# Layer 1 MLP: last four block products of a pair's second product inside the next pair's first; layer 0 issues its sum transfers at the pairs' ends

## The reference, cut to what matters

```python
def _sq_relu_mlp(h, w1, w2):
    return jnp.square(jax.nn.relu(h @ w1)) @ w2
...
        h_lat = h_lat + g1 * y_lat
        h_lat = h_lat + g2 * _sq_relu_mlp(_modulate(_rms_norm(h_lat, norm2_g[i]), sh2, sc2), mlp_w1[i], mlp_w2[i])
        if not last:
            h_ctx = h_ctx + cg1 * y_ctx
            h_ctx = h_ctx + cg2 * _sq_relu_mlp(_modulate(_rms_norm(h_ctx, norm2_g[i]), csh2, csc2),
                                               mlp_w1[i], mlp_w2[i])
```

## Time and profile before

| what | value |
|---|---|
| median of 3 runs (2562.03 to 2565.29) | 2564.84 us |
| the profiled execution: its time, its span | 2568.6 us, 2567.1 us |
| PE busy | 2319.5 us, 90% of the span |
| DVE busy | 1731.1 us, 67% |
| ACT, POOL busy | 1155.4 us, 1155.5 us, 45% each |
| mean granted TensorE clock | 0.956 |
| layer 0's MLP, pairs 0 to 15 | about 320 to 1271 us |
| layer 1's MLP, loop over pairs 2 to 15 | about 1940 to 2547 us |

### The profile page before, as it was taken

One profiled execution on the slowest core, in us unless ns is written; L12 is line 12 of the kernel. 1 busy time (PEld: TensorE's weight loads), 2 busy tenths in 40 slices (PEclk: granted clock), 3 DMA queues, 4 the chain that ended last, 5 costly groups with the idle time before them and its releaser, 6 DMA issues. The chain is left out here.

```text
span 2567.1 us, 38476 instructions
## 1 busy us (share of the span) xinstructions
PE 2319.5 (90%) x11430; PEld 1908.2 (74%) x11430; DVE 1731.1 (67%) x2827; ACT 1155.4 (45%) x2117; POOL 1155.5 (45%) x974
## 2 busy tenths in 40 slices
PE   5989989999999999999789798989988999998988
PEld 3768768888888877888677677767767777777776
DVE  5643786766776766676674688871787676767675
ACT  5543433333333333333343488883444444444444
POOL 0004533333334444433546566665455554545453
PEclk9999989999999999999889899999989999999999
DMA  7434225555544555554512211105122222222222
GB/s 264 168 136 165 99 60 159 150 139 144 134 131 131 146 144 150 160 151 108 165 61 99 93 32 38 33 21 205 38 66 73 83 82 86 86 86 86 86 80 84
DMA packets 132197, 283.51 MB, mean 110 GB/s; under 512 B 11408, under 2 KB 19984, under 8 KB 128784
## 3 DMA queue, kind: packets, MB, share of 16 engines
q1 hardware_dynamic: 111776, 242.09, 28.1%
q0 software_dynamic: 17408, 33.56, 7.9%
q10 hardware_dynamic: 2928, 6.82, 0.7%
HBM read 265.64 MB, written 83.89 MB: 136 GB/s over the span
## 5 line engine op out<-in xcount | busy, mean ns | idle before, releaser
L881 POOL TENSOR_TENSOR ht<-ht,l_side 128x512 f32<-128x512 f32 x112 | 167.5, 1495 | 535.8 <-ACT l_side L1017 533.6
L51 PE MATMUL l_z_ps<-nh,l_w1h 128*128 128x512 f32 (+1 forms) x816 | 292.9, 359 | 6.6 <-POOL l_w1l L58 3.4
L53 PE MATMUL l_z_ps<-nh,l_w1l 128*128 128x512 f32 (+1 forms) x816 | 291.8, 358 | 0.0
L52 PE MATMUL l_z_ps<-nl,l_w1h 128*128 128x512 f32 (+1 forms) x800 | 285.8, 357 | 0.0
L1321 DVE SCALAR_TENSOR_TENSOR ht<-l_yy_ps,mod,ht 128x512 f32<-128x512 f32 x336 | 235.9, 745 | 20.6 <-PE l_yy_ps L1637 19.2
L2662 PE MATMUL l_yy_ps<-l_ah,l_w2h 128*128 128x512 f32 x448 | 190.2, 425 | 61.3 <-DVE ht L2491 61.1
L58 POOL TENSOR_TENSOR l_w2l<-l_w2f,l_w2h 128x512 fp32r<-128x512 f32 x128 | 181.4, 1467 | 108.9 <-ACT l_w2h L2157 105.1
L58 POOL TENSOR_TENSOR l_w1l<-early,l_w1h 128x512 fp32r<-128x512 f32 x104 | 135.6, 1311 | 179.7 <-ACT l_w1h L2149 179.7
L1635 PE MATMUL l_yy_ps<-l_ah,l_w2h 128*128 128x512 f32 x448 | 187.0, 417 | 22.3 <-ACT l_side L1017 14.6
L3389 POOL TENSOR_TENSOR sc<-sc,den 128x640 f32<-128x640 f32 (+1 forms) x128 | 149.5, 1200 | 91.8 <-DVE den L3471 91.8
L2664 PE MATMUL l_yy_ps<-l_ah,l_w2l 128*128 128x512 f32 x448 | 185.3, 414 | 0.0
(11 more groups left out here) (338 smaller groups left out, 6533.5 us busy)
## 6 DMA issues: line engine op xcount, KB each, us to landing
l_aw<-ada SPq DMA_DIRECT2D x128, 256.0 KB, 2.9
sums<-w SPq DMA_DIRECT2D x64, 512.0 KB, 7.8
maw<-ada SPq DMA_DIRECT2D x24, 1024.0 KB, 5.1
l_w1f<-w SPq DMA_DIRECT2D x32, 512.0 KB, 5.8
l_w2f<-w SPq DMA_DIRECT2D x32, 512.0 KB, 4.2
sums<-w POOLq DMA_DIRECT2D x32, 512.0 KB, 7.3
sums<-sums POOLq DMA_DIRECT2D x32, 512.0 KB, 5.9
l_w2f<-sums SPq DMA_DIRECT2D x64, 256.0 KB, 2.7
```

Of the source, the lines that this page charges most:

```text
L51: pe.matmul(out, lh, rh, start=first, stop=False)
L52: pe.matmul(out, lh, rl, start=False, stop=False)
L53: return pe.matmul(out, ll, rh, start=False, stop=last)
L881: pool.tensor_tensor(h, h, side[(i - 1) % 2][:], ALU.add).then_inc(s_add, 1)
```

## The change: what it does

Layer 0: POOL's list for a pair is reordered. `first_sums` stands at the pair's start, behind the "S4" transfer of the pair before; "S2" stands at the pair's end. After the last pair "S4" follows at once, and POOL waits for it as before.

Layer 1: the block products with the indices 3, 4, 5 of a pair run on PE behind the next pair's first-product blocks M1, M5 and M6, index 6 behind M4. The lists of the other engines follow. Operand and weight rings have new slots and release conditions (`W2_RING`, `W2_AFTER`, `A_AFTER`), the operand order is new, DVE splits four w2 blocks per pair where it split three and POOL three where it split four. The number of matmuls, `acc`, `diff` and `low` per pair is the same. The last pair's four late products run behind the loop.

```diff
@@ -923,18 +923,18 @@
                 def outputs(p, more):
+                    if C:
+                        if type(p) is not int or p:
+                            more_sums(p - 1, "S4")
+                        first_sums(p)
                     add(p, "M5")
                     low2(p, "S2")
                     add(p, "M3")
-                    if C:
-                        first_sums(p)
                     if more and C:
                         low1(p + 1, 0)
                     low2(p, "S3")
                     for prod in ROWS[2:]:
                         add(p, prod)
-                        if C and prod in ("M2", "M7"):
-                            more_sums(p, "S2" if prod == "M2" else "S4")
...
+                    if C:
+                        more_sums(p, "S2")
...
                 outputs(PAIRS - 1, False)
                 if C:
+                    more_sums(PAIRS - 1, "S4")
                     pool.wait_ge(s_s4, 16 * PAIRS)
...
-    ON_DVE2 = 3
-    A_ORDER = ["B11", "T2", "T3", "T1", "T4", "B22", "B21"]
+    W2_RING = [0, 1, 2, 0, 1, 0, 2]
+    W2_AFTER = [(1, 5), (1, 4), (1, 6), (0, 0), (0, 1), (0, 3), (0, 2)]
+    HIGH2, DVE2, POOL2 = [1, 0, 2, 3, 4, 6, 5], [1, 0, 6, 5], [2, 3, 4]
+    A_ORDER = ["B11", "T2", "T3", "B21", "T4", "T1", "B22"]
...
@@ -2484,53 +2536,87 @@
+                def pair_start(p):
+
+                    low(p - 1, "T1")
+                    acc(p - 1, 3)
+                    low2(p - 1, 6)
+                    low(p - 1, "B22")
+                    low2(p - 1, 5)
+                    acc(p - 1, 4)
+
+                def pair(p, earlier=True):
+                    if earlier:
+                        pair_start(p)
+                    low2(p, 1)
+                    if earlier:
+                        acc(p - 1, 5)
+                    low2(p, 0)
                     zsum(p, "B11")
                     square(p, "B11")
+                    zsum(p, "B22")
                     low(p, "B11")
-                    zsum(p, "B22")
                     square(p, "B22")
                     zsum(p, "B12")
                     square(p, "B12")
                     diff(p, "T1")
-                    last_sums(p, False)
+                    diff(p, "T2")
+                    if earlier:
+                        acc(p - 1, 6, (0, 1))
+                    square(p, "B21")
...
@@ -2682,10 +2774,14 @@
-                def pair(p):
-                    for prod in Z_ORDER:
+                def pair(p, earlier=True):
+                    for k, prod in enumerate(Z_ORDER):
                         hidden(p, prod)
-                    for i in (0, 1, 2, 3):
+                        if earlier and k < 3:
+                            product(p - 1, 3 + k)
+                    if earlier:
+                        product(p - 1, 6)
+                    for i in (0, 1, 2):
                         product(p, i)
```

More of the change, by code:

```diff
@@ L2050, in low_t, with pair @@
                     lo_part(pool, lo, t_full(t, j), hi).then_inc(s_tlo[t], 1)
[L2052 to L2067, removed]
+                def pair(p, more, earlier=True):
+                    low1(p, 3)
+                    if earlier:
+                        add(p - 1, 3)
+                    low1(p, 4)
+                    if earlier:
+                        add(p - 1, 4)
+                    low1(p, 5)
+                    if earlier:
+                        add(p - 1, 5)
+                    low1(p, 6)
                     if more:
@@ L2070, in pair @@
                         low1(p + 1, 2)
-                    rest(p, more)
+                        low1(p + 1, 0)
+                    if earlier:
+                        add(p - 1, 6)
+                    low2(p, 2)
+                    add(p, 0)
+                    low2(p, 3)
+                    add(p, 1)
+                    low2(p, 4)
+                    add(p, 2)
                 def low_p(w):
@@ L2096, in _ @@
                         low1(0, 2)
+                        low2(0, 2)
                 squares(UNITS - 1)
@@ L2117, in _ @@
                 low1(2, 1)
+                low2(1, 2)
+                add(1, 0)
                 low2(1, 3)
-                add(1, 0)
                 low1(2, 2)
+                add(1, 1)
                 low2(1, 4)
[L2122 to L2126, removed]
+                for i in (2, 3, 4, 5, 6):
                     add(1, i)
-                with pool.Fori(PLAIN, PAIRS - 1) as p:
+                pair(PLAIN, True, False)
+                with pool.Fori(PLAIN + 1, PAIRS - 1) as p:
                     pair(p, True)
                 pair(PAIRS - 1, False)
+                for i in (3, 4, 5, 6):
+                    add(PAIRS - 1, i)
             @block.scalar
@@ L2348, in _ @@
                     high_t("T3", j)
-                side_read(1, 3)
-                high2(1, 6)
                 for i in (4, 5, 6):
                     side_read(1, i)
-                with act.Fori(PLAIN, PAIRS - 1) as p:
-                    start(p, True)
-                    rest(p, True)
-                    for i in (4, 5, 6):
-                        side_read(p, i)
+                pair(PLAIN, True, False)
+                with act.Fori(PLAIN + 1, PAIRS - 1) as p:
+                    pair(p, True)
                 last = PAIRS - 1
-                start(last, False)
-                rest(last, False)
+                pair(last, False)
+                high2(last, 6)
+                side_read(last, 3)
+                high2(last, 5)
                 def out_half(i):
@@ L2498, in last_sums @@
                     low(p, "T3")
-                    acc(p, 0, 0)
-                    acc(p, 0, 1)
-                    if not (type(p) is int and p == 0):
+                    acc(p, 0, (0, 1))
+                    if p:
                         square(p, "B21")
                     diff(p, "T4")
+                    acc(p, 0, (2, 3))
+                    acc(p, 1, (0, 1))
+                    low(p, "B21")
+                    acc(p, 1, (2, 3))
+                    low(p, "T4")
                     low(p, "T1")
-                    acc(p, 0, 2)
@@ L2506, in last_sums @@
[L2506 to L2507 removed]
+                    acc(p, 2)
                     low(p, "B22")
[L2509 to L2520 removed]
@@ L2522, in pair @@
-                def pair(p):
-                    for i in (0, 1, 2):
-                        low2(p, i)
+                    low2(p, 6)
+                    acc(p, 3)
+                    if p:
+                        for j in range(HK):
+                            low_t("T1", j)
+                    low2(p, 5)
+                    acc(p, 4)
+                    acc(p, 5)
+                    if p:
+                        for t in ("T3", "T4"):
+                            for j in range(HK):
+                                low_t(t, j)
@@ L2582, in _ @@
                 square(1, "B22")
-                for j in range(HK):
-                    low_t("T4", j)
-                last_sums(1, True)
-                with dve.Fori(PLAIN, PAIRS) as p:
+                plain_rest(1)
+                pair(PLAIN, False)
+                with dve.Fori(PLAIN + 1, PAIRS) as p:
                     pair(p)
+                pair_start(PAIRS)
+                acc(PAIRS - 1, 5)
+                acc(PAIRS - 1, 6)
                 for i in range(len(HALVES)):
```

300 lines of the change are left out of this document (175 added, 125 removed).

## The result

The changed kernel takes 2538.02 us, median of 4 runs (2535.28 to 2538.97), against 2565.07 (2562.03 to 2568.72): a ratio of 0.989, 95% interval 0.9874 to 0.9906.

A forecast was written before the change was run, and what follows sets the result against it. PE, busy 90% of the span, was taken as the bound, with only its waits and slow clock to win. 2568.6 - 60 (layer 0) - 45 (layer 1) = 2463.6, less 3.8 for the median: 2460 us, range 2425 to 2520.

The forecast's parts named there:

- I take no change in PE's time: Layer 0: moved transfers run beside the `l_aw` loads without delaying PE, as about 2 us of slack cover them.
- the slower rival: Layer 0: the two-slot `l_aw` load chain becomes the bound of hidden; 2598 us at twice the present landing; chance 0.03.
- part of layer 0's gain is lost to the loads: Layer 0: moved transfers delay `l_aw` or weight loads; half of each wait kept gives 2496, a quarter 2478; chance 0.14.
- The price formula of that rival: Layer 0, per pair: four load rounds, each growing with the landing, less 2 us of slack; 9.2 us at twice the landing.
- 25.5 us of slow stretches: Layer 0: PE's slow matmuls behind the `low2` waits go with those waits, 15 times 1.7 us gained.
- Layer 0, what goes: Layer 0's pairs: PE's waits for `low2` (32.4 us) and `side_read` (14.6) and the slow stretches (25.5) vanish; gain 72.5 us.
- The end of layer 0: After layer 0's last pair: "S2" and "S4" follow each other unhidden, next stage 11 us later, bounds 6 and 17.
- Layer 1: Layer 1's loop: period falls to 40.6 us, 3.2 less, without a clock drop; 45 us saved, bounds 0 and 72.
- the walk: Layer 1, PE from M4 to index 2: three banks late by 1.4 us in all, from DVE operations of 0.66 us each.
- The extra split on DVE: Layer 1: one more `low2` per pair costs nothing, or 0.8 us per pair, 11 over the loop, through SBUF contention.
- The forecast of layer 0: Layer 0 in all: 72.5 us gained, 11 lost at its end, 1.5 for restarts and small waits; 60 us less.

The follow-up runs named there:

- l0_only: The kernel before with only POOL's new list in layer 0, layer 1 as before; 2587.51 us, ratio 1.0082.
- best1: `first_back` with `low1` of the next pair's first chunk ahead of `first_sums`, and "S2" and "S4" issued earlier in the last pair; 2440.75 us, ratio 0.953.
- first_back: The changed kernel with `first_sums` alone put back behind the add of M3, "S4" still at the pair's head; 2461.17 us, ratio 0.9589.
- l1_only: The changed kernel with POOL's old list in layer 0, so only layer 1 is new; 2510.56 us, ratio 0.979.
- best2: `best1` with DVE's `acc` of index 1 in layer 1 ahead of T4's difference and the `low` of B21; 2446.36 us, ratio 0.9541.
- best3: `best2` with ACT's `side_read` of index 1 ahead of the high part of B21; 2431.52 us, ratio 0.9484.
- serial: The changed kernel with POOL waiting for "S4" to land before it issues `first_sums`; 2486.64 us, ratio 0.9703.

## Why the prediction was wrong, step by step

- **The step that failed** is "I take no change in PE's time, since I put the end of these steps some 2 us ahead of the point where outputs need them". The 2 us were about right, the runs give 1.7. What was wrong is to take the delay of the chain (load, `ada_step`, next load) as less than that: DVE's waits for `l_aw` grew from 19.9 to 99.3 us, 5.7 us per pair, and PE waited 54.2 us, 3.9 per pair, with a slow stretch behind each of 14 waits. In the pair shown the slow matmuls behind 655.31 (0.42 us against 0.23) cost about 1.6 us; in seven of 13 pairs the slow stretch is about twice as long.
- The mechanism stood in the prediction twice: as the slower rival, with 0.03, and in milder form as "part of layer 0's gain is lost to the loads", with 0.14, which ended at 2496. What was wrong is the weight. I gave the transfers' time (5.9 us each in a pair of 59) as a reason against it, and left out that the new list issues three of them back to back, because "S4" waits for "S2" ahead of `first_sums`. The bunching could have been read from the order before the result, but not its size from 5.9 us: that median mixes "S2", which took 6.0 us in the pair of the earlier trace rows, with "S4", which took 10.3 when it was issued at 617.16 among SP's copies. In the new list "S2" goes out right behind these copies, and took 10.9.
- The price formula of that rival, four rounds times the growth of the median landing less 2 us, comes out near by luck. With 4.1 us for 2.8 it gives 3.2 per pair, and 3.9 were measured. But `l0_only` has a median of 3.2 us and the same waits (54.8 us), `best1` has 3.9 and none. What holds is the growth of DVE's summed waits less the slack: 5.7 - 1.7 = 4.0.
- The rival also left out that a new wait of PE brings its slow clock with it. I had counted 25.5 us of slow stretches as gained; with the measure from above, 25.6 us before became 34.1 us, and only in `first_back` and `best1`, where PE does not wait at L1550, it is 0.
- **Layer 0, what goes**: right. The waits for `low2` went, and `first_back` and `best1` give the gain once the loads are left in peace. From 58.6 to 54.0 us in `best1` is 4.6 per pair, and the step's 72.5 us are 4.8. The 14.6 us for `side_read` hang on `first_sums` not standing ahead of `low1`: they return in `first_back`, where it does, and are gone in `best1` and in the changed kernel.
- **The end of layer 0**: right, 10.6 us against 11. From the issue of "S2" to that of "S4" it takes 6.1 us, and from there to PE's start 7.2, near the 5.9 and the 5.9 + 1.2 of the working.
- **Layer 1**: right. The period is 40.07 against the 40.6 forecast, the three late banks are where the walk has them, and the clock does not fall. One support of the last point was weak: the stretch 2028 to 2072 has its own wait of 2.33 us, at 2054.97, and is one of two pairs of 13 in which the clock stayed at 1.00 behind it; in the other eleven the mean is 0.96. The walk had PE late by 1.4 us, the trace shows 1.05 and three restarts of 0.11. So the loop gives 14 x 3.7 = 52 us of the 54 in `l1_only`. That DVE's order sets these waits is shown by `best2` only together with `best3`: taken alone it moved them and gained nothing. ACT's new order without DVE's was not tried.
- **The extra split on DVE.** By the Trainium skill, "SBUF — State Buffer", section "Who interferes with whom", an operation of DVE with both inputs in SBUF contends with POOL's reads of SBUF. The prediction put 11 us on it, if it showed. The trace agrees with the rule: the splits of w2 blocks on DVE in the loop had a median of 0.68 us before (42 of them) and have 1.37 now (56 of them, POOL at work beside those that I looked at). The period shows no price for it, because DVE waits in that stretch anyway, 1.17 us for ACT ahead of the split at 2086.24. The prediction's "0.69 in most rows" for its own example was wrong, though: the low parts made from `l_slot` had a median of 1.10 us before.
- The forecast of layer 0 taken term by term with what was measured (from 300 us to the last matmul of layer 0's MLP, then the gap): PE's waits went from 63.0 to 71.4 us, the gap grew by 10.6, and what the clock lacks grew from 39.3 to 46.0. That makes +25.7 where the trace has +23.1; the 2.6 left are open.
- What also stays open is how the DMA engines share themselves between POOL's queue and SP's. That the loads land late when POOL's transfers are issued just ahead of them is shown; which rule of sharing does it was not tried, nor whether bytes or packets count.

## What to carry to other kernels

A step moved "into idle time" of its engine moves its DMAs too: write down what else is issued in that stretch, and above all whether a wait inside the moved block bunches transfers that had been spread out. What a chain of loads with two buffers costs is the sum of its waits less the slack at its end, not the median landing: `serial` has a longer median than the changed kernel (4.6 against 4.1 us) and is 51 us faster. So measure the slack first, here by the waits at which PE began to stand still. And a wait that is removed by reordering one engine's list is not gone until the next engine in line has been looked at: the gain of `best2` showed only when ACT's list followed.

## What the runs showed of the hardware

- 1.5 MB issued by POOL with accumulation kept all 16 DMA engines busy for about ten microseconds, mostly at 160 to 260 GB/s with SP's loads in it, and a load of 256 KB issued by SP right behind took 6.9 us where the median before was 2.8.
- PE's clock was at 0.57 in the 4 us behind a wait of 3.20 us (656 to 660), and at 1.00 from 660 to 666; before, it was at 0.59 behind a wait of 1.98 us (670 to 674). The length of a wait alone does not decide it: behind waits of 2.33 us in layer 1 before it fell in eleven pairs of 13 and stayed at 1.00 in two. Waits of 0.7 to 1.7 us, one in 55, as in `first_back`, and three of 0.3 us in 40, as in layer 1 now, left it at 1.00 throughout.
